# Output-gate projection moved from the prompt attention program to between the cache products, gates on four column groups, cache copies redistributed

## The reference

```python
h = _rmsnorm(x, prm['g_pre1']) * (1 + sc1) + sh1
parts = jnp.split(h @ prm['w_in'], split_points, axis=-1)
qk, conv_new = _causal_conv(parts[0], conv_s, prm['conv_w'], prm['conv_b'])
qk = jax.nn.silu(qk)
vm = heads(parts[1])
ipre = (parts[3] + prm['b_igate']).astype(f32).transpose(0, 2, 1)
logf = jax.nn.log_sigmoid((parts[4] + prm['b_fgate']).astype(f32)).transpose(0, 2, 1)
hm, C1, n1, m1 = _mlstm_chunkwise(qm, km, vm, ipre, logf, C0, n0, m0)
hm = hm.transpose(0, 2, 1, 3) * jax.nn.sigmoid(parts[2].astype(f32)).reshape(B, L, M_HEADS, M_HEAD_DIM)
...
# for each sample and each of three windows (128, 512, 2048): attention over the cache
new_buf = jnp.stack([ek[:, -Wb:], ev[:, -Wb:]], axis=2)
```

## Time and profile before

| what | value |
|---|---|
| median of the 3 runs shown | 2501.39 us (2500.7 to 2506.66) |
| profiled execution | 2500.45 us, its span 2498.7 us |
| PE busy | 2168.8 us (87%) |
| PEld busy | 1251.7 us (50%) |
| DVE busy | 1228.3 us (49%) |
| ACT busy | 764.2 us (31%) |
| POOL busy | 734.8 us (29%) |
| DMA | 875.53 MB, mean 350 GB/s |

### The profile page before, as it was taken

How to read it: one execution, slowest core, us unless ns; L and a number is a source line. 1 busy time by engine, 2 the same in 40 slices (tenths; PEclk the granted TensorE clock), 3 DMA queues, 4 the chain that set the end, 5 groups by cost and what they waited for, 6 DMA issues and landing times.

```text
span 2498.7 us, 25279 instructions
## 1 busy us (share of the span) xinstructions
PE 2168.8 (87%) x9074; PEld 1251.7 (50%) x9074; DVE 1228.3 (49%) x3177; ACT 764.2 (31%) x2200; POOL 734.8 (29%) x694
## 2 busy tenths in 40 slices
PE   6999989997799879999997878787879787978786
PEld 3777438874588545555553433343334333433221
DVE  1000001216233146566566766767676766676864
ACT  2000012242132034444234443343333333333322
POOL 0000001110102013434333535344434343435351
PEclk8999989997699989999998989898989898989899
DMA  9566648988686649999999999999999999999997
GB/s 355 224 250 236 249 151 306 329 315 325 252 306 223 224 183 390 391 404 399 393 389 394 420 398 400 419 416 409 420 419 413 420 418 412 382 420 420 420 420 299
DMA packets 125490, 875.53 MB, mean 350 GB/s; under 512 B 15945, under 2 KB 17257, under 8 KB 40501
## 3 DMA queue, kind: packets, MB, share of 16 engines
q0 software_dynamic: 85760, 691.32, 68.7%
q1 hardware_dynamic: 38652, 182.48, 19.3%
q10 hardware_dynamic: 952, 0.13, 0.0%
HBM read 861.53 MB, written 99.37 MB: 385 GB/s over the span
## 4 chain that ended last, share of the span: by engine, by line
PE 35%; DVE 14%; DMA 13%; ACT 2%; issue 2%; POOL 0%; ACTq 0%; POOLq 0%; DVEq 0%
PE ps L1868 24%; DMA pr_ring<-in_uv,pr_idx 12%; PE ps L1764 3%; DVE pr_ring L2090 3%; PE ps L1804 3%; PE ps L1813 1%; PE ps L1826 1%; PE ps L1786 1%; DVE pr_hot L2074 1%; DVE pr_hot L2070 1%; DVE pr_ind L2051 1%; DVE pr_ind L2048 1%; DVE pr_pick L2077 1%; DVE pr_val L2050 1%; ACT pr_coef L1940 1%
## 5 line engine op out<-in xcount | busy, mean ns | idle before, releaser
L1868 PE MATMUL ps<-pr_ring,pr_diag 128*128 128x512 f32 (+1 forms) x2224 | 1042.4, 623 | 209.6 <-ACT pr_diag L1944 209.4
L1749 POOL DMA_INDIRECT pr_ring<-in_uv,pr_idx x556 | 640.6, 1152 | 956.0 <-PE ps L1868 812.0
L2090 DVE CUSTOM_DVE_ANT_0 pr_ring<-pr_ring,h 128x1024 f32<-128x1024 f32 x556 | 662.7, 1224 | 353.6 <-DMA pr_ring<-in_uv,pr_idx 351.2
L1868 PEld LDWEIGHTS ps<-pr_ring,pr_diag 128*128 128x128 f32 (+1 forms) x2224 | 424.4, 195 | 772.9 <-issue 476.7
L1935 ACT ACTIVATE pr_gel<-pr_dots 128x2 f32<-128x2 f32 x288 | 58.0, 201 | 521.7 <-DVE pr_dots L2090 521.0
L1944 ACT ACTIVATE pr_diag<-ident,pr_coef 128x128 f32<-128x128 f32 x512 | 173.5, 386 | 0.0
L1940 ACT ACTIVATE pr_coef<-pr_gel,pr_wgt 128x1 f32<-128x1 f32 x576 | 138.4, 287 | 27.0 <-ACT pr_gel L1935 0.4
L1764 PE MATMUL ps<-trunk,pr_wq 128*128 128x320 f32 (+2 forms) x544 | 132.1, 397 | 3.0 <-ACT trunk L1970 2.2
L465 PE MATMUL ps<-trunk,ap_ring 128*128 128x288 f32 x384 | 126.5, 411 | 2.9 <-PEq L192 2.9
L379 DVE TENSOR_TENSOR late_rows<-ps,late_bias 128x512 f32<-128x512 f32 x2 | 1.4, 692 | 253.0 <-PE ps L369 253.0
L466 PE MATMUL ps<-trunk,ap_ring 128*128 128x288 f32 x384 | 125.6, 409 | 0.0
(11 more groups left out here) (316 smaller groups left out, 2255.5 us busy)
## 6 DMA issues: line engine op xcount, KB each, us to landing
out_win_s<-in_cache POOLq DMA_DIRECT2D x64, 1020.0 KB, 7.9
sa_ring<-in_cache SPq DMA_DIRECT2D x24, 1024.0 KB, 9.4
side_unit<-in_w_merge SPq DMA_DIRECT2D x32, 768.0 KB
late_ring<-in_w_ada SPq DMA_DIRECT2D x8, 2048.0 KB, 17.3
sa_ring<-in_kcacheB SPq DMA_DIRECT2D x16, 1024.0 KB, 7.7
pr_wq<-in_peer_wq SPq DMA_DIRECT2D x16, 1024.0 KB
out_win_s<-in_cache POOLq DMA_DIRECT2D x16, 1008.0 KB, 9.8
ap_ring<-in_w_attn_qk SPq DMA_DIRECT2D x6, 2048.0 KB, 21.2
```

Source lines behind the costliest of these rows:

```text
L1749: pool.indirect_dma_start(row(n), None, d["uv"], bass.IndirectOffsetOnAxis(ap=idx[:, b % 4, j:j + 1], axis=0)).then_inc(arrived[slot(n)], 16)
L1868: mm = pe.matmul(ps[0:r, bank + half, :], diag[:, slot(n), 0:r], row(n)[:, o:o + CHUNK], start=h == 0 and j == 0, stop=b == FINAL[i] and j ...
L2090: ins = dve.tensor_tensor_reduce(u, u, e.h2[:, BLOCKS[b][0], :], 1.0, 0.0, ALU.mult, ALU.add, dots[:, slot(n):slot(n) + 1])
```

## The change

Three things change.

1. The ten output-gate pieces leave the prompt attention program (`self.loads` is 6 instead of 8, `first_pieces` is `[2] * 4 + [1] * 2 + [0] * 10`). They are now computed in `conv_and_gates` between the products: pieces 0 to 2 after product 1, 3 and 4 after product 2, 5 and 6 after product 3, 7 to 9 after the gate rows that follow product 4. Their two weight blocks of 1 MB go to one buffer `cg_ow`; the second is loaded when the first five pieces are done. ACT takes their sigmoids between the SiLUs of the convolutions.
2. The input and forget gates are computed by 32 matmuls of 288 columns. Four of them (gate and half of the tokens) stand on four column groups and write partitions 0, 32, 64 and 96 of one bank. Both gates are now ahead of product 0, where the second one was between products 0 and 1.
3. The cache copies: after the units of the projections one and two in turn (58 in all, before 39), and two per step of the attention (30, before 49).

```diff
@@ project, POOL @@
-                    if k.rolls:
-                        pool.wait_ge(s_mm, u + 1)
+                    pool.wait_ge(s_mm, u + 1)
+                    for _ in range(min(1 + u % 2, len(k.rolls))):
                         dst, src = k.rolls.pop()
                         pool.dma_start(dst, src).then_inc(k.s_roll, 16)
@@ MlstmProjections @@
-        self.loads = 8
+        self.loads = 6
...
-                out, how = (m.v, ACT.Copy) if n < 6 else (m.o, ACT.Sigmoid)
-                ins = act.activation(out[0:r, j, o:o + self.WIDE], res[0:r, 0:self.WIDE], how)
+                ins = act.activation(m.v[0:r, j, o:o + self.WIDE], res[0:r, 0:self.WIDE], ACT.Copy)
@@ prompt_attention @@
-        first_pieces = [2] * 4 + [1] * 12
+        first_pieces = [2] * 4 + [1] * 2 + [0] * 10
...
-                    for _ in range(min(3 if s else 4, len(k.rolls))):
+                    for _ in range(min(2, len(k.rolls))):
@@ conv_and_gates @@
+GATES = ((1, 0), (1, 1), (0, 0), (0, 1))
...
+        ow = placed(nc, "cg_ow", [P, KD, WIDE], k.keep + 4 * T * 5)
...
                 sa.load(sp, range(sa.SR))
+                sp.dma_start(ow[:], d["w_mlstm"][6]).then_inc(ow_ready, 16)
                 sp.dma_start(smask[:].rearrange("p q n -> p (q n)"), d["c_smask"]).then_inc(sa.s_mask, 16)
                 sa.load(sp, range(sa.SR, 4 * sa.PARTS))
+                sp.wait_ge(s_om, NCH)
+                sp.dma_start(ow[:], d["w_mlstm"][7]).then_inc(ow_ready, 16)
                 sp.wait_ge(s_new, 2)
...
-                for gate in (1, 0):
-                    for part, cols in ((0, slice(0, SEQ)), (1, slice(SEQ, T))):
-                        n = cols.stop - cols.start
-                        for c in range(KD):
-                            mm = pe.matmul(ps[0:H, 2 * gate + part, 0:n], wg[:, c, gate * H:(gate + 1) * H],
-                                           k.hT[:, c, cols], start=c == 0, stop=c == KD - 1)
-                    mm.then_inc(s_gm, 1)
-                    sa.product(pe, 1 - gate)
-                for n in range(2, 5):
-                    sa.product(pe, n)
+                def output_gate(u):
+                    j = u % NCH
+                    if j == 0:
+                        pe.wait_ge(ow_ready, 16 * (u // NCH + 1))
+                    if u >= 3:
+                        pe.wait_ge(s_ot, u - 2)
+                    for c in range(KD):
+                        mm = pe.matmul(ps[0:tile_rows(j), 1 + u % 3, 0:WIDE], k.hT[:, c, tile_cols(j)], ow[:, c, :],
+                                       start=c == 0, stop=c == KD - 1)
+                    mm.then_inc(s_om, 1)
+
+                for step in range(KD):
+                    for j, (gate, half) in enumerate(GATES):
+                        mm = pe.matmul(ps[32 * j:32 * j + H, 0, 0:TH], wg[:, step, gate * H:(gate + 1) * H],
+                                       k.hT[:, step, half * TH:(half + 1) * TH], start=step == 0, stop=step == KD - 1)
+                mm.then_inc(s_gm, 1)
...
+                for u in range(7, 2 * NCH):
+                    output_gate(u)
                 for n in range(5, NS):
                     sa.product(pe, n)
...
+                def output_gates(us):
+                    for u in us:
...
+                        act.wait_ge(s_om, u + 1)
+                        act.activation(m.o[0:r, j, o:o + WIDE], ps[0:r, 1 + u % 3, 0:WIDE], ACT.Sigmoid).then_inc(s_ot, 1)
...
-                for b in range(H):
-                    silu(b)
+                silu(0)
+                silu(1)
+                output_gates(range(0, 3))
+                silu(2)
+                silu(3)
+                output_gates(range(3, 5))
                 act.wait_ge(s_rows, 1)
...
+                output_gates(range(5, 7))
+                silu(4)
+                silu(5)
+                output_gates(range(7, 2 * NCH))
+                silu(6)
+                silu(7)
```

More of the change, by code:

```diff
@@ L961, in conv_and_gates @@
         wg = sb("cg_wg", [P, KD, 2 * H])
[L962 removed]
+        gb = sb("cg_gb", [P, 2])
         m0 = sb("cg_m0", [H, NS])
@@ L1012, in _ @@
                 pe.wait_ge(s_in, 7 * 16)
[L1013 to L1022 removed]
+                def output_gate(u):
[13 more added lines that the diff above has]
+                mm.then_inc(s_gm, 1)
+                sa.product(pe, 0)
+                sa.product(pe, 1)
+                for u in range(0, 3):
+                    output_gate(u)
+                sa.product(pe, 2)
+                for u in range(3, 5):
+                    output_gate(u)
+                sa.product(pe, 3)
+                for u in range(5, 7):
+                    output_gate(u)
+                sa.product(pe, 4)
                 pe.wait_ge(s_exp, 1)
```

31 lines of the change are left out of this document (20 added, 11 removed).

## The result

The changed kernel takes **2507.73 us** (median of 20 runs, 2497.93 to 2520.11). The kernel before takes 2497.89 us in the same session (20 runs, 2487.19 to 2506.66). The ratio is 1.0041, 95% interval 1.0027 to 1.0056: some 10 us slower, where the prediction said 15 us faster.

A forecast was written before the change was run, and what follows sets the result against it. It took PE to bound the projections and attention, and conv and gates to be half bound by DMA. -32 + 14.7 + 2 = -15.3 us from the median of 2501.39 gave 2486 us, range 2470 to 2502.

The forecast's parts named there:

- 1, attention, -32: Attention program: ten output-gate pieces fewer save 34.8 us of PE, less 2.4 of waits and 0.4 of hand-overs: 32 us saved.
- 2, gates, nothing: Conv and gates: column-grouped gates free 11.5 us of PE, but cache loads still set the second product's end, so none shows.
- 3, output gate between the products, +14.7: Conv and gates: pieces between products leave DMA idle with a full ring; stage 14.7 us longer, bounds 3 and 35.
- 4, cache copies, +2: Projections: 19 more copies delay the `late_ring` load; PE waits 0 to 1.5 us at about six loads, 2 us lost (0 to 11).
- Rival D: Projections: copies make the single-slot `late_ring` load late, 10 to 24 us over six loads; 2499 us in all; chance 0.12.
- Rival C: Conv and gates: output-gate pieces run at half clock, 6.9 us instead of 3.45 each; 2514 us in all; chance 0.10.
- Rival B: Conv and gates: the output-gate pieces fit into PE's waits, stage only 3 us longer; 2474 us in all; chance 0.18.

The follow-up runs named there:

- copies_alone2: Kernel before with only the new cache-copy schedule (one and two in turn in the projections, two per attention step); ratio 1.0049 to before.
- spread_gap: Changed kernel with extra copies in the gaps of the `late_ring` load, output-gate pieces spread by ones and twos behind products, gate weights loaded later; 2472.79 us, ratio 0.9894.
- late_first: Changed kernel with the `late_ring` load issued as soon as its slot is free, ahead of the wait for an `ap_ring` slot; 2486.19 us, ratio 0.9947.
- gates_alone2: Kernel before with only the input and forget gates changed: four column groups, both ahead of product 0; ratio 0.9985 to before.
- three_last: Changed kernel with extra copies in the gaps of the `late_ring` load and output-gate pieces 7 to 9 behind the last product; 2482.17 us, ratio 0.9924.

## Why the prediction was wrong

It forecast 2486 us, -15; measured is 2508, +10. By its own steps:

- **1, attention, -32: right**, measured -34.6. Of these 2.4 are the border behind the stage, which the new copy schedule gives without the moved pieces too (1.4 us in `copies_alone2`); the steps themselves gave 32.2. The last four waits in front of a value product are 0.31 us at most and not 0.6. What it missed has no effect on the number: that the border would have cost 21.1 with the old copies.
- **2, gates, nothing: right.** PE needs 4.24 us for them (4.3 forecast). Product 1 ends 31.4 us after the stage's start and not 28.5, since DMA moved less than the 411 GB/s I took (365 in the 10 us from 573).
- **3, output gate between the products, +14.7: the mechanism right, the size off**, measured +20.6 (17.6 to 26 by which profiles are compared). The miss is 2.9 us at the end of product 1; then 2.2 for the gate rows (8.3 instead of 6), which run at a clock of 0.56, and 2.0 for the three pieces behind them (12.5 instead of 10.5), which start at it. The rest comes out 1 us shorter than forecast; the idle DMA before product 5 is there. The stage ended within the bounds of 3 to 35. The granted clock is 0.79, where I said near 0.85.
- **4, cache copies, +2: the step that failed**, measured +20.2, nearly twice the upper bound. The price of a copy was good: in the median the load lands 6.2 us later (23.5 against 17.3) with two copies more beside it, 3.1 us each, where I had 2.8. It had counted five copies instead of three beside the load, too, but charged the load with "one or one and a half" of the two new ones and let no load land later than 24 us. Four of the six waits are in fact 0.2 to 1.4 us, inside its 0 to 1.5. The step failed at the other two: loads that land after 26.8 and 29.1 us, with a sixth copy issued beside them after 23.2 and 20.5 us, and PE waits 4.0 and 8.9 us for them, 12.9 of the 15.8 in all. For the second it also took the wrong time in hand: 20.1 us, as in the kernel before, and not 22.8. And it had no term for what follows a wait of that length: the clock falls, and the products behind the two take 3.50 and 3.64 instead of 1.95 us, 3.2 us more. The border has the last 1.0 (8.4 against 7.4).

**Rival D** named this mechanism: a single-slot load that the copies make late, 10 to 24 us in six places, 2499 in all. Its total holds here: 20.2 us in the projections, of which six waits are 15.8. Its single waits (1.7 to 4 us at each) don't: four are shorter and one is 8.9. With D at 20 and the stage at 20.6 the sum is -34.6 + 20.6 + 20.2 = +6.2; 3.9 us more stand in the program ahead, whose instructions did not change, and 0.7 in those behind. That is the +10.8 of the spans. D got a chance of 0.12 only. It was the likelier reading of the earlier trace rows: the load had 3.9 us to spare at its slowest (and 2.7 where it had 20.1 us in hand), and two more copies of 2.8 us each were put beside it.

**Rival C** is false: a piece takes 3.85 us on average (38.5 by ten), under the 4.5 that it needed. The changes between full and column-grouped matmuls show no loss either: in `spread_gap` two pieces between two products take 7.17 us, where one takes 3.62 in the attention. **Rival B** is false in the kernel as changed, since the pieces left 21.9 us of waits as they were; the spread versions come near it (+1 to +12 us in the stage), once most products are followed by as much work as the next one's loads need. Its reason against, that three slots let DMA run ahead by one product only, was right: it is what sets how much may stand behind one product.

## What to carry to other kernels

Before traffic without a deadline is added to a stage, look up the slowest landing of every load with a single slot, and what it is issued behind; with 3.9 us to spare, issue it first or keep the other traffic away from the moment of its issue; either brought the projections back to 317.1 to 318.4 us here. Work moved into a stage that waits for loads is hidden only in portions as long as a refill of the ring, one behind each product: ten pieces cost 18 to 26 us in blocks of 3, 2, 2 and 3, and 1 to 12 in portions of two or one (the spread version also puts the gate weights' loads later and no piece beside the gate rows, so what the portions alone are worth was not measured). A stage that gets shorter in front of a program border must have its DMA over by then, too, or the border takes the gain.

## What the runs showed of the hardware

**A load behind another on one queue.** With the `late_ring` load 0.4 us behind the `ap_ring` load, the medians are 10.5 and 17.3 us before and 13.5 and 23.5 after the change: the second lands 7 to 10 us behind the first. 8 us apart, as in `late_first`, they are 9.2 and 13.5. What made the load at 260.23 take 29.1 us stays open in part: in `copies_alone2` the same load, with the same six copies beside it, takes 26.0, and from 260 to 290 all queues together kept the DMA engines busy 89% of the time, not all of it.

**The same instructions take 7 us more or less by when the clock rises.** The mLSTM program is the same in all kernels. It takes 194.0 to 197.3 us in eight of the thirteen profiles and 201.7 to 203.4 in five. Its first and second 20 us, in the kernel before and then in `gates_alone2` (columns as in the windows above):

```profile
665.10:685.10 20.00, 19.68 (x232) 16.30 (x236) 8.78 (x33) 5.26 (x12) 3.23 (x7) 0.74 0.50 187
685.10:705.10 20.00, 20.00 (x213) 16.85 (x201) 5.16 (x22) 7.24 (x14) 0.00 (x0) 1.00 0.75 261
```

```profile
665.30:685.30 20.00, 19.68 (x80) 16.93 (x80) 4.57 (x14) 2.83 (x7) 3.22 (x7) 0.50 0.48 185
685.30:705.30 20.00, 20.00 (x218) 16.04 (x219) 7.94 (x33) 5.93 (x13) 0.00 (x0) 0.81 0.59 211
```

PE is busy all the time in both, after 8.6 us of idle time at the border in both, and the first 20 us have 232 records of matmuls in the one and 80 in the other. In all five long ones the first 20 us stand at 0.50 to 0.51, in the other eight at 0.73 to 0.76. The program ahead of the projections shows the same, at 42.6 to 51.1 us. What decides it no run here tells; the idle time at the border doesn't, for the long ones stand behind 3.7, 5.8 and 8.6 to 8.9 us of it and the short ones behind 6.1 and 8.4 to 8.9. Whether `three_last` and `spread_gap` lose their 8 us there in every run, or only in the profiled one, stays open. It is the reason to compare stages, and to give no weight to a few us of a single stage or span.
